# A two-layer decoder trunk: experts' results summed in four PSUM banks, raw rows gathered with a factor per slot, a gate weight in freed rows, a shorter warm-up

## The reference

```python
for layer in range(DEPTH):                      # 2
    hn = rms_norm(h, norm_mix[layer])
    mix = attention(hn) if layer % 2 == 0 else hgrn2(hn)
    h = h + mix
    h = h + hier_moe(rms_norm(h, norm_ffn[layer]), ...)
return rms_norm(h, final_norm)

def hier_moe(x, ...):                           # per token: 2 experts, weights in combine
    hid = silu(einsum('sd,edf->sef', x, w_gate)) * einsum('sd,edf->sef', x, w_up)
    return einsum('sef,efd->sd', hid * combine[..., None], w_down)

def rms_norm(x, gain):
    return x * rsqrt(mean(x * x, -1) + EPS) * gain
```

## Time and profile before

| | |
|---|---|
| median of 3 runs | 728.1 us (727.38 to 729.61) |
| the profiled execution | 732.78 us, its span 731.1 us |
| busy | PE 624.0 us (85%), PEld 411.3, DVE 300.8, ACT 242.6, POOL 35.2 |
| HBM read | 242.82 MB, mean 334 GB/s over the span |
| attention, layer 0's experts | 0 to 159 us, 159 to 367 us |
| recurrence, layer 1's experts | 367 to 514 us, 514 to 722 us |

### The profile page before, as it was taken

The page is one execution under the profiler, slowest core; times in us unless marked ns, Lnnn a source line. Parts: engine busy times, 40 slices in busy tenths (PEclk is TensorE's granted clock), DMA queues, the critical chain, the costliest instruction groups (busy, mean ns, idle before and its releaser), DMA issues.

```text
span 731.1 us, 11097 instructions
## 1 busy us (share of the span) xinstructions
PE 624.0 (85%) x4490; PEld 411.3 (56%) x4490; DVE 300.8 (41%) x518; ACT 242.6 (33%) x540; POOL 35.2 (5%) x64
## 2 busy tenths in 40 slices
PE   8999899999997595675989999999999976595775
PEld 7997787776542341322269987887754431341321
DVE  3756687524232211312285698652522330221304
ACT  4545556442211110100157685662411110110112
POOL 3020000000000100000000001060000000000000
PEclk9999999999999888977999999999999998897989
DMA  8949336799999999999996636579989999999993
GB/s 325 274 123 340 114 117 208 306 403 360 401 422 392 410 420 421 421 422 422 405 388 220 231 128 218 185 265 403 386 358 392 416 422 422 422 421 421 421 415 142
DMA packets 59712, 244.52 MB, mean 334 GB/s; under 512 B 4545, under 2 KB 8913, under 8 KB 38930
## 3 DMA queue, kind: packets, MB, share of 16 engines
q1 hardware_dynamic: 58400, 242.33, 84.5%
q0 software_dynamic: 768, 1.40, 0.8%
q10 hardware_dynamic: 498, 0.15, 0.1%
HBM read 242.82 MB, written 1.05 MB: 334 GB/s over the span
## 4 chain that ended last, share of the span: by engine, by line
PE 54%; DMA 31%; DVE 5%; SPq 5%; ACT 2%; issue 2%; DVEq 0%; POOL 0%; POOLq 0%; ACTq 0%
DMA ring<-in_moe_w_down 31%; PE psum L2278 7%; PE psum L1849 6%; PE psum L2223 6%; PE psum L1860 3%; PE psum L1853 3%; SPq L541 3%; PE psum L1851 3%; PE psum L1858 3%; PE psum L2216 3%; PE psum L2358 2%; PE psum L2360 2%; PE psum L2359 2%; SPq L508 2%; PE psum L1816 1%
## 5 line engine op out<-in xcount | busy, mean ns | idle before, releaser
L2223 PE MATMUL psum<-ring,xT 128*32 128x512 f32 x512 | 66.9, 679 | 33.5 <-DMA ring<-in_moe_w_up 33.5
L2223 PE MATMUL psum<-arena,xT 128*32 128x512 f32 x512 | 63.9, 657 | 34.6 <-DMA arena<-in_moe_w_up 34.6
L1567 DVE TENSOR_TENSOR arena<-psum,arena 128x256 f32<-128x256 f32 x16 | 6.8, 425 | 210.3 <-ACT arena L1051 210.3
L2278 PE MATMUL psum<-ring,arena 128*32 128x512 f32 x456 | 61.8, 626 | 14.4 <-DMA ring<-in_moe_w_down 14.3
L1047 ACT ACTIVATE arena<-psum 128x256 f32<-128x256 f32 x16 | 6.1, 383 | 202.0 <-PE psum L2223 202.0
L2216 PE MATMUL psum<-arena,xg 128*128 128x128 f32 x512 | 61.5, 277 | 0.8 <-DVE arena L1553 0.8
L2216 PEld LDWEIGHTS psum<-arena,xg 128*128 128x128 f32 x512 | 59.3, 193 | 2.7 <-issue 2.7
L2223 PEld LDWEIGHTS psum<-arena,xT 128*32 128x32 f32 x512 | 16.9, 120 | 76.8 <-issue 41.2
L2223 PEld LDWEIGHTS psum<-ring,xT 128*32 128x32 f32 x512 | 16.9, 123 | 76.0 <-issue 41.1
L2207 PE MATMUL psum<-xT,arena 128*128 128x512 f32 x128 | 57.7, 594 | 0.0
L1849 PE MATMUL psum<-x_hi,w_hi 128*128 128x256 f32 x224 | 56.0, 288 | 1.7 <-DVE x_hi L1252 1.2
(11 more groups left out here) (341 smaller groups left out, 1050.2 us busy)
## 6 DMA issues: line engine op xcount, KB each, us to landing
ring<-in_moe_w_down SPq DMA_DIRECT2D x54, 1024.0 KB, 20.1
ring<-in_moe_w_gate SPq DMA_DIRECT2D x32, 1024.0 KB, 15.5
ring<-in_moe_w_up SPq DMA_DIRECT2D x32, 1024.0 KB, 17.7
arena<-in_moe_w_gate SPq DMA_DIRECT2D x32, 1024.0 KB, 20.7
arena<-in_moe_w_up SPq DMA_DIRECT2D x32, 1024.0 KB, 22.6
ring<-in_rec_w_in SPq DMA_DIRECT2D x16, 1024.0 KB, 13.7
ring<-in_att_w_in SPq DMA_DIRECT2D x8, 1024.0 KB, 10.7
ring<-in_att_w_out SPq DMA_DIRECT2D x4, 1024.0 KB, 14.7
```

The lines of the kernel that those rows point to most:

```text
L2223: return pe.matmul(bank(3)[e * CAP:(e + 1) * CAP, :].rearrange("p (w f) -> p w f", w=2), gatheredT[:, k, e * CAP:(e + 1) * CAP], w, start= ...
L2278: last = pe.matmul(bank(5 + c)[e * CAP:(e + 1) * CAP, :], hidT[:, j, e * CAP:(e + 1) * CAP], down_part(l, kind, e, j)[:, c * 512:(c + 1) * ...
```

## The change

Seven things change.

1. Sums in PSUM. Banks 0 to 3 belong to the sums of the two tiles through all of a layer's experts. `start_sums` puts h there by four products with the identity, in the body of quad 2 behind its gather; every combine adds to them, and `add_rows` is gone. The norm after the experts reads the sums in PSUM (`sum_bank`, `row_sum`), and in layer 0 h itself is copied back later. The gather moves to banks 4 and 5, which it shares with `down`, and so waits for the copies of y of quad n - 2 (`busy`).
2. Raw rows. The gather takes the rows of h, not of xg; `scaled_rows` is gone. Two products of one column give each slot its token's norm factor (`rate_psum`), ScalarE copies it with its sign turned (`slot_rate`), and silu takes it as its scale: exp of the gate's product, and both multiplications on VectorE.
3. A gate weight in xg. The freed tile xg holds expert 0's gate weight of quad 2, loaded by `load_in_x` while the mixer runs; the product of that expert is split in two of 256 columns.
4. Chunks 0 and 1 of quad 0 both run before the second half of its gather.
5. Between the layers: the transposes go to banks 4 to 7, x_low of t = 0 goes ahead, the first recurrence product is taken in three parts with a wait each (`first_three`), the lower bounds are made ahead of the last rows.
6. Warm-up: START 16 to 6, FIRST 4 to 2; `ident` is made before `ones`.
7. The last output goes out as one tile and two halves.

```diff
-        START, FIRST, ROUTE, NORM = 16, 4, 19, 10
+        START, FIRST, ROUTE, NORM = 6, 2, 19, 10
-        COMBINE_BANKS = (7, 2, 0, 1)
+        SUM_TILES = ((0, 0), (0, 1), (1, 0), (1, 1))
+        LAST_TILES = ((0, 0), (1, 0), (0, 1), (1, 1))
+        GATHER, GATE_UP, TURN, FIRST_RATE = 4, 6, 7, 3
...
+        def load_in_x(sp, l, *free):
+            sp.wait_ge(*free)
+            sp.dma_start(x_weights, moe_w_gate[l].rearrange("(q e) (p r) f -> q e p (r f)", e=QE, p=P)[2][0])\
+                .then_inc(s[f"gate_up_loaded{l}_0"], 16)
...
                     load_lent(sp, 0, 0, s["xg_done"], TT)
+                    load_in_x(sp, 0, s["proj_psum"], 12)
                     sp.wait_ge(s["sb_pv"], SB_H)
...
                     load_gate_up(sp, 1, 1, 1, 1, (0,))
+                    load_in_x(sp, 1, s["rec_psum"], rows_done(3, 1))
                     sp.wait_ge(s["ko_psum"], 4)
...
-                    load_gate_up(sp, l, 2, 0, e)
+                    load_gate_up(sp, l, 2, 0, e, (0, 1) if e else (1,))
...
-                        if t == 0:
-                            scaled_rows(v, 0)
...
-                scaled_rows(v, 1)
...
+            def slot_rate(l, n, parity, small=False):
+                act.wait_ge(s[f"rate_psum{l}"], n + 1)
+                act.activation(rate[:, parity:parity + 1], rate_psum(small), ACT.Copy, scale=-1.0)\
+                    .then_inc(s[f"gatheredT{l}"], 1)
...
+            def start_sums(l):
+                for done in (f"y_front{l}", f"y_back{l}", "passes_ready"):
+                    pe.wait_ge(s[done], l + 1 if done == "passes_ready" else 1)
+                for half, t in SUM_TILES:
+                    pe.matmul(sum_bank(half, t), ident[:, :], h[:, t, half * 512:(half + 1) * 512],
+                              start=True, stop=False, skip_group_check=True)
...
-                    pe.matmul(bank(b), shareT[:, t, :], y_rows[:, half * 512:(half + 1) * 512],
-                              start=True, stop=True).then_inc(s[f"combined{l}"], 1)
+                    pe.matmul(sum_bank(half, t), shareT[:, t, :], y_rows[:, half * 512:(half + 1) * 512],
+                              start=False, stop=last, skip_group_check=True)\
+                        .then_inc(s["h_done" if last else f"combined{l}"], 1)
...
+                    if busy and k % 4 == 0:
+                        pe.wait_ge(s[f"y_back{l}" if k else f"y_front{l}"], n - 1)
+                    if k == KD - 1:
+                        for t in range(TT):
+                            col = pe.matmul(rate_psum(small), slots[:, t].rearrange("p e c -> p (e c)"),
+                                            norm_rstd[:, v, t:t + 1], start=(t == 0), stop=(t == TT - 1))
+                        col.then_inc(s[f"rate_psum{l}"], 1)
...
-            def later_gate_up(l, n, parity):
+            def later_gate_up(l, n, parity, in_x=False):
...
+                        if in_x and e == 0:
+                            for i, part in enumerate((lent, w[0][:, 1])):
+                                pe.matmul(bank(GATE_UP)[0:CAP, i * FF:(i + 1) * FF], gatheredT[:, k, 0:CAP],
+                                          part[:, k, :], start=(k == 0 and i == 0), stop=(k == KD - 1),
+                                          skip_group_check=True)
...
-                pe.wait_ge(s[f"added{l}"], 4 * n - 4)
-                gather(l, n)
+                gather(l, n, busy=not early)
+                if early:
+                    start_sums(l)
...
-                gather(l, 0, between=lambda: first_gate_up(l, 0), first=True)
-                for c in range(1, KD // 2):
+                gather(l, 0, between=lambda: [first_gate_up(l, c) for c in range(KD // 4)], first=True, small=True)
+                for c in range(KD // 4, KD // 2):
...
+                    for t in range(TT):
+                        dve.tensor_copy(h[:, t, :], row_sum(t)).then_inc(s["h_kept"], 1)
```

More of the change, by code:

```diff
@@ L370, in half_parts, with turned_bank @@
             return hi[:, m % 2], w_lo[:, RING_SLOT[base + m // 2], :, m % 2 * 256:(m % 2 + 1) * 256]
+        def turned_bank(v, t, half):
+            return bank(2 * t + half + (4 if v == 2 else 0))
         def rec_turned(part, b):
@@ L376, in gather_bank @@
         def gather_bank(k, first):
-            return bank(2) if first and k in (2, 3) else bank(k // 4)
+            if first:
+                return bank(2) if k in (2, 3) else bank(k // 4)
+            return bank(GATHER + k // 4)
         def rows_hi(p):
@@ L430, in hybrid_trunk @@
         hidT = a(KF, P)
+        rate = a(2)
         a.at = tail + RH * T
@@ L1245, in norm @@
                 dve.wait_ge(s["gain_loaded"], 8 * v)
-                dve.scalar_tensor_tensor(out=xg[:, t, :], in0=h[:, t, :], scalar=norm_rstd[:, v, t:t + 1],
-                                         in1=gain[:, :], op0=ALU.mult, op1=ALU.mult)\
-                    .then_inc(s["xg_done"], 1)
+                halves = (slice(0, D),) if v < 2 * NL or t == 0 else (slice(0, D // 2), slice(D // 2, D))
+                for c in halves:
+                    dve.scalar_tensor_tensor(out=xg[:, t, c], in0=row_sum(t)[:, c], scalar=norm_rstd[:, v, t:t + 1],
+                                             in1=gain[:, c], op0=ALU.mult, op1=ALU.mult).then_inc(s["xg_done"], 1)
             def xT_half(v, t):
@@ L1592, in experts @@
                 place(l, 1)
-                silu(l, 0)
+                silu(l, 0, 0)
                 gathered(l, 1, 1)
@@ L1596, in experts @@
                 place(l, 2)
-                silu(l, 1)
-                rows(l, 0)
+                silu(l, 1, 1)
+                rows(l, 0, first=True)
                 with dve.Fori(1, NQ // 2 - 1) as i:
-                    body(l, 2 * i, 2 * i, 2 * i + 1)
-                    body(l, 2 * i + 1, 2 * i + 1, 2 * i + 2)
+                    body(l, 2 * i, 2 * i, 2 * i + 1, 0)
+                    body(l, 2 * i + 1, 2 * i + 1, 2 * i + 2, 1)
                 more = dve.value_load(passes[l][0:1, 0:1], min_val=0, max_val=PASS_MAX - 1)
@@ L1860, in three, with first_three @@
                         last = pe.matmul(dst, a_hi(k), b_lo(k), start=False, stop=(k == KD - 1))
+                return last
+            def first_three(dst, ready, a_hi, a_lo, b_hi, b_lo, a_first):
+                for k in range(KD):
+                    pe.matmul(dst, a_hi(k), b_hi(k), start=(k == 0), stop=False)
+                pe.wait_ge(s["w_low_dve"], LOW_DVE["rec"] + 1)
+                for k in range(KD):
+                    pe.matmul(dst, a_lo(k), b_hi(k), start=False, stop=False)
+                pe.wait_ge(*ready)
+                for k in range(KD):
+                    last = pe.matmul(dst, a_hi(k), b_lo(k), start=False, stop=(k == KD - 1))
                 return last
@@ L2257, in turn_hidden, with down @@
                 for j in range(KF):
-                    last = pe.transpose(bank(4)[:, j * P:(j + 1) * P], hid[:, j::KF], ident[:, :])
+                    last = pe.transpose(bank(TURN)[:, j * P:(j + 1) * P], hid[:, j::KF], ident[:, :])
                 last.then_inc(s[f"hid_psum{l}"], 1)
-            def down(l, n, last_quad=False, early=False):
+            def down(l, n, last_quad=False, early=False, first=False):
                 pe.wait_ge(s[f"hidT{l}"], n + 1)
@@ L2277, in down @@
                         for e in range(QE):
-                            last = pe.matmul(bank(5 + c)[e * CAP:(e + 1) * CAP, :],
+                            last = pe.matmul(down_bank(c, first)[e * CAP:(e + 1) * CAP, :],
                                              hidT[:, j, e * CAP:(e + 1) * CAP],
```

215 lines of the change are left out of this document (113 added, 102 removed).

## The result

The changed kernel takes **758.6 us** (median of 4 runs, 756.5 to 760.9) against 728.9 (4 runs, 727.4 to 732.4): ratio 1.040, interval 1.036 to 1.043. The forecast was 731.7 us, the range 725.5 to 737.0: **wrong** in size, 27 us too low. The profiled execution took 758.75 us, its span is 757.0.

A forecast was written before the change was run, and what follows sets the result against it. The prediction took the experts' weight stream to be the bound, once TensorE's earlier work lets it run without gaps. Terms -3.1 + 4.0 - 0.3 + 4.0 - 1.0 = +3.6 us on 728.1 gave 731.7 us, range 725.5 to 737.0.

The forecast's parts named there:

- the reserve: Stream slack before quad 2's down weights are issued: 19.9 us of loads against 18.0 us of waiting, 1.9 us.
- The gate weight in xg: Quad 2's early gate weight, loaded into freed rows: value 0, bounds 0 and -2.5 us per layer.
- Work ahead of B: Before quad 3's loads are issued at quad 1's gate/up end (B): 0.9 stall plus 0.8 rate columns, 1.7 us later.
- B to C: From quad 3's gate/up load issue to quad 2's down-weight issue: 18.0 becomes 22.2 us, opening a 2.3 us hole per layer.
- start of the sums: Quad 2's body: four identity products with h, priced like a combine, add 3.4 us.
- Split: Quad 2's body: expert 0's gate/up product in two halves costs one pass, 0.4 us; other bound 3.4.
- Start: Kernel start: the shorter warm-up brings the projection's first product earlier, -3.1 us, gain capped at 4.6.
- Between the layers: Passage between layers: norm from PSUM and reordered VectorE work complete x_lo sooner, -0.3 us, bounds +0.5 and -1.5.
- End: Kernel end: earlier norm of t = 1 and a last output of half the bytes, -1.0 us, bounds -0.5 and -2.
- the split: Rival, slower: quad 2's split product holds the tiles up, 3.0 us more per layer, 737.7 us; chance 0.10.
- the megabyte: Rival, faster: the early gate weight saves 2.5 us per layer with sums hidden, 718.7 us; chance 0.08.
- A low clock behind routing: Slower rival: low TensorE clock after routing; chance 0.10, its size not in the text given.

The follow-up runs named there:

- the second of before: Kernel before, unchanged, profiled once more: execution 727.24 us, span 725.5 us.
- The blocks: Changed kernel with gathers reading 128 adjacent channels of h instead of every eighth, output not the reference's: 973.6 us, layer 1 routing other rows.
- the combination: Changed kernel with ScalarE's scaled rows in gather order, residual added in quad 3, no per-slot norm factor or early gate weight, old first-gather order: 726.0 us, ratio 0.996.

## Why the prediction was wrong, step by step
- **The step that failed:** "The stationary operand of a gather is now a strided view of h. A turn of h with the same stride loads its weights in 190 ns and the gather in 193, so that is free." It is 334 ns, and a gather takes 8.1 - 0.34 - 3.57 = 4.2 us more. Two gathers lie between E and B and one between B and C, where the reserve is gone already: 3 x 4.2 = 12.5 us a layer, 25 in all, nearly the 27 us by which the forecast was short. (Between the changed kernel's profile and the second of before lie 31.5 us where +3.6 were forecast; of the 27.9 that are missing, 25.1 lie in the two layers and 2.8 in start, passage and end.) The blocks gave 11.7 back in a layer and the stride in the kernel before cost 10.2 and 11.0 (there the reserve still took 1.9). The row used as evidence belonged to a transpose, an operation of another form. It should have been one end of a range, whose other end no row showed.
- *The gate weight in xg:* value 0, right.
- *Work ahead of B:* the stall, 0.9 forecast, is 0.85 us; the rate column, 0.4 forecast, 0.34. The low clock behind the stall, 0.66 in the window from 180 to 185 us, cost 1.7 us in layer 0 (5.34 for 3.64) and was not in the sum.
- *B to C:* start of the sums 3.4, measured 3.44. Split 0.4, measured 7.02 against 7.00 us for the whole group, nothing: the three other experts start at 220.48, 0.45 us ahead of the second half that the program puts before them, and the 3.4 us of the other bound did not come. That the hole adds in full behind an exhausted reserve held within about 0.5 us in every run that had a hole: 6.1 in the changed kernel, 2.2 with the stride alone, 1.6 with the start of the sums in quad 2 of the combination.
- *Start:* -3.1 forecast. No run shows the 3.1 us as the worth of the short warm-up; the pairs of runs with and without it lie 0.07% (0.5 us) to 0.36% (2.6 us) apart. Against the profile shown the first product moved from 17.11 to 13.81, with the gain product at 3.78 us where it took 1.98. Against the second profile it moved by 0.3. VectorE's two multiplies ahead of the turns took 2.47 us in both profiles of before, at granted clocks down to 0.50 in the one and of 1.00 in the other. **The second fault is the yardstick:** that execution lay 4.7 us above the median, and 3.0 of these sat in the very stretch that the term was taken from. The saving was subtracted from a median that need not have had the loss: the execution of 727.24 us did not.
- *Between the layers:* -0.3 forecast, -0.6 measured, the same against either profile of before. *End:* -1.0 forecast, -1.5.
- *Rivals:* the split is refuted by its run and by the trace. The sign given for it, C - B over 24 us, came all the same (26.0): it could not tell the split from a slower gather. The condition of the megabyte, a B early enough for the stream, never came about. A low clock behind routing came in layer 0 and cost 1.7 us there. None had the operand's price, so the range didn't either.

## What to carry to other kernels
Price an access pattern by a row of the same operation, passes and operand role; the transpose's 190 ns said nothing about the product's 334. Keep a float32 stationary operand's elements at most 8 bytes apart, as far as these runs go (196 ns a load at 8, 329 at 16): two copies in ScalarE that put a layer's rows in order are what lets each of its 8 gathers take 3.57 us instead of 7.7 us. And before a saving is taken off the median, see whether the profiled execution is one that the median stands for.

## What the runs showed of the hardware
- A load of a 128x128 float32 stationary operand takes 193 to 196 ns with a step of 4 or 8 bytes, and 329 to 336 ns with 16 or 32. Passes that follow each other then come every 0.25 us instead of 0.11.
- Such passes with a step of 32 bytes hardly slow down at the lower clock: 16 take 4.05 us at a granted clock of 1.00 and 4.16 at 0.59, while 16 passes on adjacent elements took 2.02 at 1.00 and 3.56 at 0.58 to 0.50.
- A transpose on TensorE with a step of 32 bytes is one pass of 0.13 us; the same rows turned by a plain product are two passes of 0.25 us.
- Products in different 32-column strips kept 0.88 us a step when one of the four was split in halves: 7.02 us for eight steps, 7.00 unsplit. The trace has the other three started at 220.48 us, ahead of the second half that stands before them in the program (220.93).
- Four banks that stay open for a sum over a whole stage cost nothing by themselves in layer 0: E to D is 164.3 us with them and 164.4 without.
- Executions of the unchanged kernel spread from 726.8 to 733.4 us, with mean clocks from 0.948 to 0.937; the shorter ones tend to have the higher clocks.
